# Gate columns by themselves in float32, and denominators summed as columns, in a two-block kernel

## The reference

```
gates = (rmsnorm(x, g) @ w_in)[:, 3072:3080] + gate_b      # 4 input, 4 forget
b = cumsum(log_sigmoid(fg))                                # per head
h = num / max(|den|, exp(-m));  h = h * rsqrt(mean(h*h) + eps)
# second block: c = cumsum(log_sigmoid(f + b_f)), f = eight columns of w_in
```

## Time and profile before

| what | value |
|---|---|
| median of three runs | 1872.8 us |
| the profiled execution | 1873.61 us, its span 1871.9 us |
| TensorE busy | 1841.0 us, 8914 matmul records |
| VectorE, ScalarE, POOL busy | 930.5, 742.4, 275.6 us |
| mean granted TensorE clock | 0.995 of full |
| DMA | 93 GB/s over the span |

### The profile page before, as it was taken

How to read it: one execution, slowest core, us unless ns; L and a number is a source line. 1 busy time by engine, 2 the same in 40 slices (tenths; PEclk the granted TensorE clock), 3 DMA queues, 4 the chain that set the end, 5 groups by cost and what they waited for, 6 DMA issues and landing times.

```text
span 1871.9 us, 21712 instructions
## 1 busy us (share of the span) xinstructions
PE 1841.0 (98%) x8914; PEld 1502.1 (80%) x8914; DVE 930.5 (50%) x1439; ACT 742.4 (40%) x1184; POOL 275.6 (15%) x241
## 2 busy tenths in 40 slices
PE   9999999999999999999999999999999999999998
PEld 7877778888888887787888888878877788888886
DVE  6667555452444456635544345466666433323324
ACT  5646344331232446644433133442557333212223
POOL 2000222220121200002221022112001122201210
PEclk9999999999999999999999999999999999999999
DMA  6122122323222332212232322231121222222221
GB/s 224 68 96 74 45 97 83 113 91 112 90 90 96 107 125 101 91 46 100 81 113 90 111 93 84 91 117 68 68 91 46 84 97 90 102 101 90 95 92 62
DMA packets 31666, 173.89 MB, mean 93 GB/s; under 512 B 3392, under 2 KB 5568, under 8 KB 13648
## 3 DMA queue, kind: packets, MB, share of 16 engines
q1 hardware_dynamic: 26320, 163.03, 24.5%
q10 hardware_dynamic: 5248, 9.47, 1.6%
HBM read 170.36 MB, written 2.13 MB: 92 GB/s over the span
## 4 chain that ended last, share of the span: by engine, by line
PE 90%; DVE 5%; ACT 3%; issue 1%; DMA 1%; POOL 0%; SPq 0%; DVEq 0%; ACTq 0%; POOLq 0%
PE ps L941 51%; PE ps L1185 18%; PE ps L885 7%; PE ps L960 5%; PE ps L1096 2%; PE ps L1051 2%; PE ps L1076 1%; DVE WL L1659 1%; PE ps L1135 1%; DMA raw<-in_wall 1%; PE ps L1116 1%; ACT PB L1412 1%; ACT WH L1258 1%; PE ps L865 0%; PE ps L874 0%
## 5 line engine op out<-in xcount | busy, mean ns | idle before, releaser
L941 PE MATMUL ps<-hH,WH 128*128 128x512 f32 x1472 | 580.2, 394 | 3.8 <-DVE WL L1659 1.3
L941 PE MATMUL ps<-hH,WL 128*128 128x512 f32 x1472 | 573.1, 389 | 0.0
L941 PE MATMUL ps<-hL,WH 128*128 128x512 f32 x1472 | 573.0, 389 | 0.0
L1659 DVE TENSOR_TENSOR WL<-raw,WH 128x1024 fp32r<-128x1024 f32 (+2 forms) x312 | 382.9, 1267 | 362.5 <-ACT WH L1258 362.4
L1258 ACT ACTIVATE WH<-raw 128x1024 fp32r<-128x1024 f32 (+2 forms) x312 | 303.4, 1020 | 288.2 <-PE ps L1185 228.7
L941 PEld LDWEIGHTS ps<-hH,WH 128*128 128x128 f32 x1472 | 276.4, 188 | 67.5 <-issue 8.4
L941 PEld LDWEIGHTS ps<-hL,WH 128*128 128x128 f32 x1472 | 276.4, 188 | 58.9 <-issue 2.6
L941 PEld LDWEIGHTS ps<-hH,WL 128*128 128x128 f32 x1472 | 276.3, 188 | 58.0
L1185 PE MATMUL ps<-fH,WH 128*128 128x512 f32 x528 | 205.4, 389 | 0.0
L1185 PE MATMUL ps<-fL,WH 128*128 128x512 f32 x528 | 205.4, 389 | 0.0
L1185 PE MATMUL ps<-fH,WL 128*128 128x512 f32 x528 | 205.4, 389 | 0.0
(11 more groups left out here) (336 smaller groups left out, 1997.3 us busy)
## 6 DMA issues: line engine op xcount, KB each, us to landing
raw<-in_wall SPq DMA_DIRECT2D x140, 1024.0 KB, 4.6
raw<-in_wall SPq DMA_DIRECT2D x12, 768.0 KB, 4.0
bias<-in_bias ACTq DMA_DIRECT2D x12, 256.0 KB, 3.3
X<-in_xt SPq DMA_DIRECT2D x8, 256.0 KB, 9.6
CB<-rows ACTq DMA_DIRECT2D x8, 256.0 KB, 3.4
out_y<-X SPq DMA_DIRECT2D x3, 512.0 KB, 3.0
raw<-in_wall SPq DMA_DIRECT2D x4, 256.0 KB, 5.6
mrA<-in_memt ACTq DMA_DIRECT2D x4, 256.0 KB, 6.3
```

The lines of the kernel that those rows point to most:

```text
L941: mm = e.matmul(ps[b][:, 0:N], ww[:, k, c:c + 128], x[:, k, 0:N], start=(k == 0 and i == 0), stop=(k == 7 and i == 2))
L1659: e.tensor_tensor(WL[n % NCV][:, c], raw[n % NRAW][:, c], WH[n % NCV][:, c].bitcast(F32), ALU.subtract).then_inc(*mark("wl", n, x))
```

## The change

1. The gate columns leave the weight plan. They come as a small input `gatew`: for each block 8 x 8 numbers per partition (`graw`), and a 128 x 8 matrix `gsum` that picks and adds rows. VectorE multiplies them by the norm's weights into `gw` (eight tiles of 32 columns, of which 8 are filled). "gate_products" is eight float32 matmuls of gw with X itself, tile k going to output partitions 32(k mod 4) on: four groups of partitions, each with the sum of two products. Eviction multiplies all 128 partitions by Rsb; a matmul with gsum adds the four groups.
2. "gates_rest" is cut in two; the cumulative sum comes 3 tiles after the eviction, the rest 4. The input gates come by a second matmul, into a bank of their own.
3. In m_den POOL adds the denominators' squares to the values' squares. m_sums handles a pair of heads: sums as columns (tokens on partitions), clamp, root and reciprocal on 128 x 8 numbers, eight pieces of a diagonal; m_norm spreads each by one matmul and multiplies out of PSUM. m_den moves ahead of m_prep 3, and a tile moves between m_sums and m_norm of the second pair.
4. Second block: a dv unit takes the gate unit's place, and the final residual's products (x_final) move to the dk tiles.

```diff
-    u += [("a_w_in", 0, 0, 8, 3072, 128), ("a_w_in", 0, 0, 8, 3080, 256)]
+    u += [("a_w_in", 0, 0, 8, 3080, 256)]
...
-    u += [("w_in_2", 0, 0, 8, 0, 256), ("w_in_2", 0, 0, 8, 2952, 128)]
-    u += [("w_in_2", 0, 0, 8, 256 * j, 256) for j in (1, 2, 3, 4, 5, 6, 8, 10, 7, 9, 11)]
+    u += [("w_in_2", 0, 0, 8, 256 * j, 256) for j in (0, 4, 1, 2, 3, 5, 6, 8, 10, 7, 9, 11)]
...
-            timed.extend([[1, ("gates_later",)], [2, ("gates_rest",)], [5, ("gate_columns",)], [6, ("m_rows",)]])
+            timed.extend([[1, ("gates_later",)], [2, ("gates_sums",)], [3, ("gates_rest",)], [5, ("gate_columns",)], [6, ("m_rows",)]])
...
+    put("gate_weights", "A")
     for k in range(8):
         put("scaled", "mix0", k, None)
...
     rstd("mix0", 60)
-    fm(1, "mix0", "gate", "gate")
+    put("gate_products", "A")
+    waiting.append(("gate",))
     fm(1, "mix0", "qmA", "R")
...
     put("m_values", 0)
     put("m_values", 1)
-    put("m_prep", 3)
-    fill(gens, 1)
     put("m_den", 0)
     put("m_den", 1)
-    fill(gens, 1)
+    put("m_prep", 3)
+    fill(gens, 2)
     put("m_sums", 0)
-    put("m_sums", 1)
     fill(gens, 1)
     put("m_norm", 0)
     put("m_norm", 1)
...
     put("m_sums", 2)
-    put("m_sums", 3)
     for t in range(3):
         put("gated", t)
+    fill(gens, 1)
     put("m_norm", 2)
     put("m_norm", 3)
...
+    put("gate_weights", "C")
     ffn(1, "ffn1", None)
...
+    put("gate_products", "C")
+    waiting.append(("fg",))
     fm(1, "n1", "dq", "rope")
-    fm(1, "n1", "fgate", "fg")
+    tm(1, "n1", "dv", "v")
     fm(1, "n1", "dq", "rope", m0=2)
-    fm(2, "n1", "dk", "rope")
-    for j in range(2):
-        for i, _ in enumerate(g_tm(1, "n1", "dv", "v", u0=j)):
-            put("x_final", 4 * j + 2 * i)
-            put("x_final", 4 * j + 2 * i + 1)
+    for i, _ in enumerate(g_fm(2, "n1", "dk", "rope")):
+        put("x_final", i)
+    for i, _ in enumerate(g_tm(1, "n1", "dv", "v", u0=1)):
+        put("x_final", 4 + 2 * i)
+        put("x_final", 5 + 2 * i)
...
+                elif what == "gate_products":            # TensorE
+                    b, before = bank("gates" + a[0], ("gate",) if a[0] == "A" else ("fgG",))
...
+                    w.wait_ge(*at("gwD", a[0]))
+                    for k in range(8):
+                        if a[0] == "A":
+                            w.wait_ge(s_x[k] if ev.sems else None, 16)
+                        else:
+                            w.wait_ge(*at("xf", 1, 1, k))
+                        r = slice(32 * (k % 4), 32 * (k % 4) + 32)
+                        mm = e.matmul(ps[b][r, :], gw[:, k, :], X[:, k, :], start=(k < 4), stop=(k >= 4))
...
-                    e.matmul(ps[b][0:4, :], ident[0:8, 4:8], O[0:8, 0, :], start=True, stop=True).then_inc(
+                    e.matmul(ps[b][0:4, :], gsum[:, 4:8], O[:, 0, :], start=True, stop=True).then_inc(
                         *mark("gates", "f"))
+                    b, before = bank("gi", ("gateD", "i"))
...
+                    e.matmul(ps[b][0:4, :], gsum[:, 0:4], O[:, 0, :], start=True, stop=True).then_inc(
+                        *mark("gates", "i"))
...
-                    e.matmul(ps[b][:, :], ones, msq[hd % 2][:, :], start=True, stop=False)
...
-                    e.matmul(ps[b][:, :], ones, den[hd % 2][:, :], start=False, stop=True).then_inc(*mark("msums", hd))
+                    for hd in (h0, h0 + 1):
+                        w.wait_ge(*at("msqS", hd))
+                        sums(b, msq[hd % 2], 4 * (hd - h0), ("msums", hd))
+                elif what == "m_norm":
...
+                    e.matmul(ps[b][:, :], ones, fac[hd % 2][:, :], start=True, stop=True).then_inc(*mark("mspread", hd))
...
+                elif what == "m_den":                    # POOL
...
+                    e.tensor_tensor(msq[hd % 2][:, :], msq[hd % 2][:, :], den[hd % 2][:, :], ALU.add).then_inc(
+                        *mark("msqS", hd))
...
             e.dma_start(K[:, :, :], consts.rearrange("p (i c) -> p i c", i=5)).then_inc(s_K, 16)
+            e.dma_start(gsum[:, :], gatew[:, 64:72]).then_inc(s_gw, 16)
+            e.dma_start(graw[:, :, :], gatew[:, 0:64].rearrange("p (k c) -> p k c", k=8)).then_inc(s_gw, 16)
             load(1)
```

More of the change, by code:

```diff
@@ L708, in program @@
         CB = [place(f"CB{i}", [128, 512]) for i in range(2)]
+        gw = place("gw", [128, 8, 32], offset=227840)
+        gsum = place("gsum", [128, 8], offset=228864)
+        graw = place("graw", [128, 8, 8], offset=228896)
         m_rows = nc.dram_tensor("m_rows", (8, 512), F32, kind="Internal").ap()
@@ L820, in last_part @@
             return 1 if n else 3
-        drains = {"mkcp": "mkv", "mvcp": "mkv", "gate": "gate", "R": "linR", "conv_in": "cvin", "o": "linR",
-                  "v": "vev", "g": "fg", "u": "fz", "fg": "fgG", "rope": "ropeU"}
+        drains = {"mkcp": "mkv", "mvcp": "mkv", "R": "linR", "conv_in": "cvin", "o": "linR",
+                  "v": "vev", "g": "fg", "u": "fz", "rope": "ropeU"}
         BANK, FREED = {}, {}
@@ L1194, in tensor @@
                         w.wait_ge(*at(*before))
-                    w.wait_ge(*at("fgG", "fgate", 0))
-                    e.matmul(ps[b][0:8, :], ident[96:128, 120:128], Gf[96:128, :], start=True, stop=True).then_inc(
-                        *mark("fgates"))
+                    w.wait_ge(*at("fgG"))
+                    e.matmul(ps[b][0:8, :], gsum[:, :], Gf[:, :], start=True, stop=True).then_inc(*mark("fgates"))
                 elif what == "lam_later":
@@ L1258, in scalar @@
                     e.activation(WH[n % NCV][:, c], raw[n % NRAW][:, c], ACT.Copy).then_inc(*mark("wh", n, x))
+                elif what == "gate_weights" and a[0] == "C":
+                    w.wait_ge(*at("gwD", "A"))
+                    e.dma_start(graw[:, :, :], gatew[:, 72:136].rearrange("p (k c) -> p k c", k=8)).then_inc(s_gw, 16)
                 elif what == "sqrt_table":
@@ L1718, in vector @@
                     diagonal("join", small[:, 32:36], ("rcol", "n1"))
+                elif what == "gate_weights":
+                    if a[0] == "A":
+                        w.wait_ge(s_cols if ev.sems else None, 16)
+                        w.wait_ge(s_gw if ev.sems else None, 32)
+                        w.wait_ge(*at("gw0"))
+                    else:
+                        w.wait_ge(s_gw if ev.sems else None, 48)
+                        w.wait_ge(*at("glin", "A"))
+                    g = (col("mix0", 0, 8) if a[0] == "A" else gg[:, :]).rearrange("p (k c) -> p k c", c=1)
+                    e.tensor_tensor(gw[:, :, 0:8], graw[:, :, :], g.broadcast_to([128, 8, 8]), ALU.mult).then_inc(
+                        *mark("gwD", a[0]))
                 elif what == "gate":
-                    name, m = a
-                    w.wait_ge(*at("lin", name, m))
+                    w.wait_ge(*at("glin", "A"))
                     w.wait_ge(*at("Rsb", "mix0"))
-                    times_R(O[0:8, 0, :], ps[BANK[(name, m)]][0:8, :], rows=slice(0, 8)).then_inc(
-                        *mark("gate", name, m))
+                    times_R(O[:, 0, :], ps[BANK["gatesA"]][:, :]).then_inc(*mark("gate"))
                 elif what == "gates_later":
@@ L1733, in vector @@
                         *mark("gateD", "abs"))
-                elif what == "gates_rest":
+                elif what == "gates_sums":
                     w.wait_ge(*at("gateA", "ln"))
@@ L1995, in vector @@
                 elif what == "fg":
[L1996 to L1997 removed]
+                    w.wait_ge(*at("glin", "C"))
                     w.wait_ge(*at("Rsb", "n1"))
[L1999 to L2000 removed]
+                    times_R(Gf[:, :], ps[BANK["gatesC"]][:, :]).then_inc(*mark("fgG"))
                 elif what == "fg_later":
@@ L2382 @@
     consts, rope = shape_constants()
+    gates = [w.reshape(8, 128, 8).transpose(1, 0, 2).reshape(128, 64)
+             for w in (z["a_w_in"][0][:, 3072:3080], z["w_in_2"][0][:, 3072:3080])]
+    group = np.tile(np.concatenate([np.eye(8, dtype=np.float32), np.zeros((24, 8), np.float32)]), (4, 1))
     arrays = {
@@ L2386 @@
         "cols": cols, "bias": bias, "consts": consts, "rope": rope,
+        "gatew": np.concatenate([gates[0], group, gates[1]], 1),
     }
```

80 lines of the change are left out of this document (50 added, 30 removed).

## The result

The changed kernel takes **1866.8 us** in the median (1864.9 to 1867.25), the kernel before 1872.93 beside it (1870.98 to 1873.47): ratio 0.9967, 95% interval 0.9956 to 0.9978. That is 6.1 us faster; 9.65 were forecast, to 1863.2. In a second series it was 1866.72 against 1872.68, 0.9966 (0.9952 to 0.9979). The profiled execution took 1864.9 us with a span of 1862.8, so 2.1 lie around the span and not 1.7; that of before lay at the high end of its runs and this one is the lowest of its own, so the two profiles differ by more (8.7) than the medians.

The account below looks back on a forecast made before the run. TensorE, busy 98% of the 1871.9 us span, was taken as the bound. Start +0.75, denominators -6.9 and second block -3.5 summed to -9.65: 1863.2 us to be measured (chance 0.50), range 1857 to 1869.5.

Parts of the forecast that it names:

- (a): Rival, start: TensorE keeps its lead of 3.5 us, q3 starts at 86; 3.5 + 0.75 better, 1859.0; chance 0.22.
- (b): Rival, gate products: one after the other, 0.86 us each; start 3.4 us more, second block 2.1; 1868.7; chance 0.14.
- Start: forecast +0.75: Start to memory heads: TensorE's lead of 3.5 us is eaten, q3 starts at 90.4 against 89.65, 0.75 us slower.
- the 1.3 us for the two DMA issues: Start: gsum and graw come ahead of raw 1 on SP's queue, making all up to 1.3 us later; 1.3 taken.
- Denominators: forecast -6.9: Recurrent heads: the pause at 232.68 and the slow clock behind it go, 6.9 us gained, bounds 2 and 7.4.
- TensorE asks at 173.5. So 0 to 0.5 us, I take 0: First pair of heads: diagonals done at 173.4, so TensorE's wait before the spread is put at 0.
- POOL's two additions: Denominators: POOL gets two additions of some 1.3 us per pair of heads.
- Rival (c): Denominators: the pause only moves, new steps are late in both pairs; 2 us won instead of 6.9; 1868; chance 0.09.
- Second block: forecast -3.5: Second block's start: 3.7 us lost waiting for X 7, gate tile's 5.5 and a 1.67 us diagonal wait won.
- The reordering of dv and dk costs nothing: the ropes run beside tiles: Second block: the new unit order was put at no cost, with scores starting two tiles behind the last dk.
- 2.9 us for eight products: Gate products: by the Trainium skill's 2.38 times, about 2.9 us instead of 2.0; sum some 0.9 higher, all in second block.
- (d): Rival, gate products: slower than before, each costing more than alone and warm, from 1.12 us on; half clock 1882; chance 0.05.

Follow-up runs that it names:

- experiment 2: The kernel before with the gate products of the start and the gates' split steps alone: 1870.86 us against 1872.02, ratio 0.9994.
- Experiment 7: The changed kernel with a second tile between sums and spreads of the first pair of heads: 1863.71 us against 1872.88 for the kernel before, 0.9951.
- experiment 1: The kernel before with the denominators' part alone, both gate tiles staying: 1868.68 us against 1872.02, ratio 0.9982.
- Experiment 5: The changed kernel with the steps after the gates' eviction one tile earlier in the start: 1864.57 us against 1872.88 for the kernel before, 0.9957.
- experiment 8: The changed kernel with earlier gates' steps, second block's products behind dq0 and later first spreads: 7.0 us below the changed kernel; 2.8 faster than without the earlier steps.
- experiment 3: The kernel before with the second block's gate products and new unit order alone: 1872.31 us against 1872.02 (1.0002); again, 1871.72 against 1872.68 (0.9998).

## Why the prediction was right, and by how much each step was off

The time is inside the stated range, which had been drawn wide enough for rivals (a) and (b), and 0.8 us outside the 1861 to 1866 given for the forecast alone. It is 3.6 from the forecast and 1.9 from (b), so the time by itself tells nothing between these; the waits and stretches do. Each part below had its sign or its mechanism right, and one term in each mis-sized.

**Start: forecast +0.75, measured -0.1 at q3.** q3 starts at 89.52 against 89.65 (in the series of the experiments 1 to 3, 89.06 against 89.40 and 89.59). The mechanism came as written: Rsb behind ScalarE's 44.16 (forecast 44.9), the wait of q2 on the bias addition, 1.8 for 2.8, the second reductions at 85.10 for 86.1. VectorE's own row: idle 7.0 us before k0 (forecast 7.2), then everything in the forecast's order.

```profile
68.12 2.32 DVE L1840 SCALAR_TENSOR_TENSOR k<-sq,cols,k 128x511 f32<-128x511 f32 x3 [7.01 <-ACT k L1410]
...
79.25 0.73 DVE L1799 TENSOR_SCALAR O<-ps,cols 4x512 f32<-4x512 f32 x1
...
85.10 1.28 DVE L1851 TENSOR_REDUCE stA<-ps 128x2 f32<-128x512 f32 x2
```

Everything is 0.7 to 1.2 us earlier than forecast. The mis-sized term is the 1.3 us for the two DMA issues: they cost 0.55 each of SP's queue, but the conversion that waits for raw 1 starts at 13.26 against 13.14. Behind q3 both kernels wait for VectorE's PTA (until 104.28 before, 103.79 now), so even this -0.1 isn't what counts. Of the 2.1 us by which the profiled executions differ at the scores, 1.6 are clock (24.22 us from that wait's end to the scores, against 22.62): two kernels with the unchanged start reach them at 126.64 and 126.82, and experiment 2, in their series, at 126.50. Like with like, the start is worth -0.1 to -0.3, and the median of experiment 2 says -1.2 with an interval from -2.8 to +0.4.

**Denominators: forecast -6.9, measured -3.6 and -1.4 to -2.0.** The pause of 4.98 us and the slow clock behind it are gone, for the reason given: the conversion of a_w_out stands ahead of the norms. The windows 232 to 240 show the clock at 1.00. What was mis-sized is "TensorE asks at 173.5. So 0 to 0.5 us, I take 0": it waits 1.07. By the clock of the profile it asks at 171.5, as it reached the scores 2.1 us sooner; counted from the scores, that is the 45 us of the forecast. VectorE is what came late: it gets to the sums at 170.90, 44.5 us behind the scores, where the forecast's 171.0 is 42.5.

```profile
170.90 0.16 DVE L1958 TENSOR_SCALAR small<-ps 128x8 f32<-128x8 f32 x1
...
171.34 0.20 DVE L1961 RECIPROCAL small<-small 128x8 f32<-128x8 f32 x1 [0.28 <-ACT small L1509]
171.57 1.66 DVE L1968 TENSOR_SCALAR fac<-K,small 128x128 f32<-128x128 f32 x8
```

The forecast had POOL's two additions cost POOL alone. But VectorE's rows beside them are longer. POOL and VectorE after, then VectorE at the same two steps before:

```profile
154.54 1.29 POOL L2219 TENSOR_TENSOR msq<-msq,den 128x512 f32<-128x512 f32 x1 [1.62 <-ACT den L1502]
156.51 1.54 POOL L2219 TENSOR_TENSOR msq<-msq,den 128x512 f32<-128x512 f32 x1 [0.69 <-DVE den L1951]
...
154.55 1.83 DVE L1951 TENSOR_TENSOR den<-q 64x512 f32<-64x512 f32 x1
156.41 2.31 DVE L1923 TENSOR_SCALAR Pm<-Mb,colA 128x512 f32<-128x512 f32 x4
```

```profile
156.65 0.69 DVE L1896 TENSOR_TENSOR den<-q 64x512 f32<-64x512 f32 x1
157.37 1.28 DVE L1868 TENSOR_SCALAR Pm<-Mb,colA 128x512 f32<-128x512 f32 x4
```

These are 2.2 us more, and VectorE's next conversion starts 34.6 us behind the scores in all ten profiles with the additions and 32.4 behind them in all four without. No run moved the additions, so that they are the cause is argued from the overlap and not shown by an experiment.

Experiment 7 gives the wait back (1.3). The second pair came as forecast: no wait. Rival (c), the pause only moves, is refuted in mechanism, for 1.07 of 6.9 came back and only in the first pair; by its median alone (3.3 us won), experiment 1 would lie in the 2 to 5 us that its expectation gave (c).

**Second block: forecast -3.5, measured -2.3.** The products did what was written: the seven, a wait of 1.59 on X, the eighth, dq0 starts 4.9 us after the last down is through and doesn't wait, where before it started at once and waited 1.2 inside: 3.7 lost. The gate tile's 5.5 and the diagonal's 1.67 are won. The failed step is "The reordering of dv and dk costs nothing: the ropes run beside tiles". Their matmuls stand in TensorE's queue, and the one of dq2 waits 1.43 us for VectorE's U. VectorE had stood 4.3 us before a conversion for ScalarE's high part, and had the forget gates' steps and a scan ahead of U:

```profile
1264.66 2.36 DVE L1701 TENSOR_TENSOR WL<-raw,WH 128x1024 fp32r<-128x1024 f32 x2 [4.30 <-ACT WH L1295]
1266.94 0.41 DVE L2074 TENSOR_SCALAR g<-g 8x512 f32<-8x512 f32 x1
...
1268.64 1.21 DVE L2079 TENSOR_TENSOR_SCAN ncum<-g,g 8x512 f32<-8x512 f32 x1
1269.78 0.65 DVE L1672 SCALAR_TENSOR_TENSOR U<-ps,Rsb 128x512 f32<-128x512 f32 x1
```

3.7 - 5.5 - 1.7 + 1.4 = -2.1, for 2.3 measured. That wait is there in the profile of every kernel with the second block's change and in none without it; no kernel was run that moves it. The prediction also says that with 2.9 us for eight products its sum would be 0.9 higher, all of it here. That doesn't follow from its own times: seven products at 0.36 us (an estimate, 2.9 for eight) would be through at 1234.6, ahead of the last X at 1235.9.

**The sum.** -0.1 to -0.3, -5.0 to -5.6 and -2.3 make -7.4 to -8.2, and around the span 0.4 comes on top (2.1 against 1.7; 1.7 also in experiments 2 and 3, 1.9 in 1): -7.0 to -7.8, against -6.1 by the medians, whose interval is -4.1 to -8.2. So the forecast's excess of 3.5 is 1.3 to 1.9 in the denominators, 1.2 in the second block and 0.4 around the span, less 0.85 to 1.05 in the start; what is left, 0.9 to 1.7 us between stretches and median, is of the size by which the clock moves single runs. The medians of the parts alone (3.3 and 1.2 us faster, and for the second block 0.3 slower and 1.0 faster) agree with the whole and are too wide to divide it.

**The rivals.** (a) is refuted for this order: q3 is not at 86. Experiment 5 has about half of its 4.25 by moving the gates' steps one tile: q3 at 87.00, PTA 2.2 us sooner, of which 1.6 are lost to the clock in each of the three profiles; by the medians of experiment 8 the shift is worth 2.8. (b) and (d) fall with 0.26 us a product (2.07 for eight); with one group (b)'s 2.1 us for the second block is confirmed (2.2), and its 3.4 for the start comes out as 4.0.

## What to carry to other kernels

Narrow float32 products whose outputs fit in different quarters of the partitions cost a third of what they cost one after the other; they can read the residual itself and spare a split weight tile. A step that is put at nothing because it "runs beside tiles" is to be followed to its own instructions in the bound engine's queue, and to what stands ahead of their operands on the other engine, or slows it there: both waits that were missed are such. And where TensorE is the bound, split the span at its own landmarks, and compare stretches with the same instructions over several kernels: that tells 0.1 us where the medians don't tell 2. It doesn't replace them: the second block's 2.3 us are in every profile, and the medians of experiment 3 don't show them.

## What the runs showed of the hardware

**The same wait is followed by half clock in some executions and not in others.** The waits before the memory values near 104 us (2.5 to 2.6 us) and before the band attention's scores near 744 (2.3 to 2.4) are the same in the executions compared. Windows of before, then of the second block's gates alone (same instructions there); then of the changed kernel, and of the changed kernel again:

```profile
104.00:108.00 4.00, 3.73 (x13) 1.63 (x14) 3.93 (x13) 0.19 (x1) 0.00 (x0) 0.65 0.00 0
```

```profile
104.00:108.00 4.00, 3.78 (x21) 2.32 (x22) 3.93 (x13) 0.13 (x1) 0.00 (x0) 1.00 0.00 0
```

```profile
742.00:746.00 4.00, 2.32 (x16) 1.30 (x16) 3.93 (x11) 2.65 (x6) 0.00 (x0) 1.00 0.48 158
```

```profile
742.00:746.00 4.00, 2.41 (x6) 1.18 (x8) 3.93 (x12) 2.63 (x5) 0.00 (x0) 0.69 0.52 160
```

The granted clock is 0.65 and 0.69 (half clock for part of the window) against 1.00. It costs 1.6 us in the first place (24.22 and 24.27 from the wait's end to the scores, against 22.61 and 22.60) and 1.6 in the second (589.53 against 587.91, one kernel twice). At the end it costs 1.0 (14.05 against 13.05). Near 1432 us it costs nothing in the end: where the clock stays up (126.13 against 127.57), TensorE waits 1.3 us for POOL soon after, and the next row is longer by what this one won. So two profiles of one kernel may differ by two or three such steps, and a part worth under 2 us can't be read from one pair of spans. What decides whether the clock falls is open. A drop that falls ahead of a wait costs nothing: in the changed kernel q3 ran partly at half clock (7.2 us to the next tile, 89.52 to 96.74, where experiment 5 has 5.6), and the wait on PTA behind it was 0.6 instead of the 2.2 of its second profile, with the same end (103.79 and 103.72).

**Columns instead of rows for a reciprocal.** The reciprocal of 128 x 8 numbers takes 0.20 us, of 128 x 512 3.35; sums as columns, sixteen records of one column, take 1.70 us from start to next tile (163.82 to 165.52), as in the sums of the earlier trace rows.
